# Two dozen tiles of a decoder kernel at other on-chip addresses: small tables regrouped, one 4-byte tile added

## The reference, cut to what matters

```python
def swiglu(x, w_gate, w_up, w_down):
    return (jax.nn.silu(x @ w_gate) * (x @ w_up)) @ w_down
def reference(...):
    mem_k, mem_v = split(rms_norm(mem, mem_norm) @ w_mem_kv)
    h = x
    h = h + mlstm_layer(rms_norm(h, ln_mix0), mem_k, mem_v, ...)
    h = h + swiglu(rms_norm(h, ln_ffn0), w_gate0, w_up0, w_down0)
    h = h + mla_layer(rms_norm(h, ln_mix1), positions, mem_k, mem_v, ...)
    h = h + moe_swiglu(rms_norm(h, ln_ffn1), w_router1, we_gate1, we_up1, we_down1)
    return h
```

## Time and profile before

| | |
|---|---|
| median of three executions | 1530.54 us (1529.33 to 1535.26) |
| the profiled execution | 1527.4 us, of which 1525.6 us from the first to the last instruction (the span) |
| TensorE products busy | 1464.8 us, 96% of the span |
| TensorE weight loads (beside the products) | 1221.0 us, 80% |
| VectorE | 1211.0 us, 79% |
| ScalarE | 1050.3 us, 69% |
| GpSimd | 40.8 us, 3% |
| moved by the DMA engines | 442.02 MB, mean 290 GB/s |
| granted TensorE clock, mean | 0.987 of full |

### The profile page before, as it was taken

How to read it: one execution, slowest core, us unless ns; L and a number is a source line. 1 busy time by engine, 2 the same in 40 slices (tenths; PEclk the granted TensorE clock), 3 DMA queues, 4 the chain that set the end, 5 groups by cost and what they waited for, 6 DMA issues and landing times.

```text
span 1525.6 us, 22113 instructions
## 1 busy us (share of the span) xinstructions
PE 1464.8 (96%) x7056; PEld 1221.0 (80%) x7056; DVE 1211.0 (79%) x1584; ACT 1050.3 (69%) x1395; POOL 40.8 (3%) x83
## 2 busy tenths in 40 slices
PE   6998999999988899999999999999999999999995
PEld 5987888888886788878878878888888888887883
DVE  6957655555565689989989989989988988998993
ACT  5664644444584377887787778878778778788772
POOL 1000000000000000000000010000000000000000
PEclk9999999999998999999999999999999999999997
DMA  8554365555242469999999999999999999999990
GB/s 270 165 180 138 139 220 182 186 195 162 66 166 77 172 240 384 378 355 387 377 351 382 390 350 386 384 360 373 380 384 346 393 381 352 389 377 350 396 393 34
DMA packets 191802, 442.02 MB, mean 290 GB/s; under 512 B 8750, under 2 KB 20364, under 8 KB 191756
## 3 DMA queue, kind: packets, MB, share of 16 engines
q1 hardware_dynamic: 188636, 429.90, 77.8%
q0 software_dynamic: 3120, 11.54, 2.7%
HBM read 433.54 MB, written 7.86 MB: 289 GB/s over the span
## 4 chain that ended last, share of the span: by engine, by line
PE 90%; DVE 5%; ACT 3%; issue 1%; DMA 0%; ACTq 0%; SPq 0%; DVEq 0%
PE bank L465 86%; PE bank L1025 2%; DVE w_lo L1613 1%; ACT w_hi L1130 1%; DVE xT_lo L1655 1%; DVE aT_lo L2274 0%; PE bank L751 0%; ACT aT_hi L1519 0%; PE bank L477 0%; DMA late<-in_mem_dram 0%; PE bank L656 0%; ACT scr L1467 0%; DVE stat L1634 0%; DVE stat L1632 0%; DVE stat L1633 0%
## 5 line engine op out<-in xcount | busy, mean ns | idle before, releaser
L1613 DVE TENSOR_TENSOR w_lo<-raw,w_hi 128x1024 fp32r<-128x1024 f32 (+1 forms) x832 | 958.6, 1197 | 175.5 <-ACT w_hi L1130 160.2
L1130 ACT ACTIVATE w_hi<-raw 128x1024 fp32r<-128x1024 f32 (+1 forms) x832 | 839.9, 1043 | 216.0 <-PE bank L465 210.8
L465 PE MATMUL bank<-w_hi,xT_hi 128*128 128x512 f32 (+4 forms) x1358 | 529.7, 390 | 12.3 <-DVE w_lo L1613 4.4
L465 PE MATMUL bank<-w_hi,xT_lo 128*128 128x512 f32 (+4 forms) x1358 | 521.8, 384 | 0.0
L465 PE MATMUL bank<-w_lo,xT_hi 128*128 128x512 f32 (+4 forms) x1358 | 521.2, 384 | 0.0
L465 PEld LDWEIGHTS bank<-w_hi,xT_hi 128*128 128x128 f32 x1358 | 255.9, 188 | 63.8 <-issue 8.6
L465 PEld LDWEIGHTS bank<-w_hi,xT_lo 128*128 128x128 f32 x1358 | 255.7, 188 | 49.6
L465 PEld LDWEIGHTS bank<-w_lo,xT_hi 128*128 128x128 f32 x1358 | 256.0, 189 | 46.0
L465 PE MATMUL bank<-w_hi,aT_hi 128*128 128x512 f32 x544 | 214.1, 394 | 5.8 <-DVE aT_lo L2274 5.8
L465 PE MATMUL bank<-w_lo,aT_hi 128*128 128x512 f32 x544 | 214.1, 394 | 0.0
L465 PE MATMUL bank<-w_hi,aT_lo 128*128 128x512 f32 x544 | 211.6, 389 | 0.0
(11 more groups left out here) (354 smaller groups left out, 763.0 us busy)
## 6 DMA issues: line engine op xcount, KB each, us to landing
raw<-in_we_gate_dram SPq DMA_DIRECT2D x112, 1024.0 KB, 7.7
raw<-in_we_up_dram SPq DMA_DIRECT2D x112, 1024.0 KB, 7.9
raw<-in_we_down_dram SPq DMA_DIRECT2D x112, 1024.0 KB, 6.9
raw<-in_w_gate_dram SPq DMA_DIRECT2D x14, 1024.0 KB, 5.1
raw<-in_w_up_dram SPq DMA_DIRECT2D x14, 1024.0 KB, 5.1
raw<-in_w_down_dram SPq DMA_DIRECT2D x14, 1024.0 KB, 4.8
raw<-in_w_in_dram SPq DMA_DIRECT2D x16, 768.0 KB, 4.9
raw<-in_w_out_dram SPq DMA_DIRECT2D x8, 1024.0 KB, 5.2
```

Source lines behind the costliest of these rows:

```text
L465: return pe.matmul(o, a, b, start=start, stop=stop, skip_group_check=True, **kw)
L1130: act.activation(split_piece(w_hi, c, shape, half), raw_piece(c, shape, half), ACT.Copy).then_inc(hi_ready, 1)
L1613: dve.tensor_tensor(split_piece(w_lo, c, shape, half), raw_piece(c, shape, half), F(split_piece(w_hi, c, shape, half)), ALU.subtract).then ...
```

## The change

Three small tiles (`row_no` of 12 bytes per partition, `gate_bias` and `pos_i` of 8) are declared later, behind `stat`; a tile `line_gap` of 4 bytes, which no instruction uses, is declared behind them; in layer 0's group `qk_in` goes to the end; in the experts' group `xg` and `y_out` go in front of `onehot`. No instruction is added, removed or moved: the lists of all engines are the same row for row in both programs, and only addresses in them differ.

```diff
-        row_no = sb("row_no", [P, TB + 1])
...
-        gate_bias = sb("gate_bias", [LH, 2])
-        pos_i = sb("pos_i", [P, TB], I32)
...
         stat = sb("stat", [P, 5, 40])
+        row_no = sb("row_no", [P, TB + 1])
+        gate_bias = sb("gate_bias", [LH, 2])
+        pos_i = sb("pos_i", [P, TB], I32)
+        sb("line_gap", [P, 1])
         kmT = sb("kmT", [P, 2, S])
...
-            qk_in = sb("qk_in", [P, 2, QB, S + TAPS - 1], scope=part)
             qkT = sb("qkT", [P, QKB, S], scope=part)
...
             headsel = sb("headsel", [LH, LH, P], scope=part)
+            qk_in = sb("qk_in", [P, 2, QB, S + TAPS - 1], scope=part)
...
             ys_lo = sb("ys_lo", [P, D], F32R, scope=part)
+            xg = sb("xg", [P, D], scope=part)
+            y_out = sb("y_out", [P, D], scope=part)
             onehot = sb("onehot", [P, TB, P], F32R, scope=part)
...
-            xg = sb("xg", [P, D], scope=part)
-            y_out = sb("y_out", [P, D], scope=part)
```

## The result

The changed kernel took 1537.46 us (median of 20 executions, 1534.47 to 1541.76), the kernel before 1530.4 us in 20 executions of the same session (1527.14 to 1535.26). The ratio is 1.0044, with a 95% interval of 1.0033 to 1.0055: 6.7 us, and not no change. The profiled execution took 1536.72 us, of which 1535.0 us is the span.

What follows compares the result with a forecast made beforehand. TensorE was taken to set the pace, with 90% of the chain. The terms summed to 0.0 us (-0.7 to +0.9, to +3 without slack), so the forecast was the earlier median, 1530.5 us, range 1526.5 to 1537.

Steps and rivals of the forecast that it cites:

- four kinds: All tiles: some stay, layer 0's big ones keep remainder 32, later ones go 0 to 32, small tables 32 to 0.
- what an instruction pays for a big operand at remainder 32: The one number the sum needs: at most 1 ns per TensorE load, -5 to +5 on VectorE, -14 to +10 on ScalarE.
- 40 ns of room hides them: Down products' 544 loads per term: 188 ns each beneath products starting 228 ns apart, so priced at 0.
- The pairs: Like operations on tiles at remainder 32 and 0 in the trace before (`gm`/`km`, `late`/`xr`): load difference at most 1 ns.
- Rest: Other loads 0.3 us; split operations hidden by 3.75 us of slack, else 2.8 us; layer 1's mixer 0.5 us; gather and scatter 0.
- Rival A: Weight loads from big tiles at remainder 32 run at half rate: 42 us more, 1572 us, 122 more at worst; chance 0.03.
- Rival B: Operands fetched in 64-byte units, so loads at remainder 32 touch nine, not eight: 6.3 us more, 1536.8 us; chance 0.03.
- Rival C: Per-partition scalars from tables at remainder 32 cost 15 ns more, now saved: 2.2 us less, 1528.3 us; chance 0.02.
- Rival D: Big tiles reach multiples of 64 after all, layer 0's going 32 to 0: worth 0, at most 0.3 us; chance 0.01.
- lines of 16 bytes: On-chip memory lines by the skill: starts at 32 and 0 cost the same, making the 64-byte-unit rival's 6.3 us nothing.

Runs made afterwards that it cites:

- e1: The changed kernel without the 4-byte tile, against the kernel before: 1530.65 us, ratio 0.9993.
- e4: The kernel before with a 4-byte tile ahead of `raw`, so every tile stands 32 bytes further: 1532.3 us, ratio 1.0004 to the kernel before.
- m1: TensorE alone, 784 products of the down product's form in 53 groups differing only in addresses: 226.7 ns for `xT`'s, 228.9 and 233.2 for `aT`'s before and after.
- m2: TensorE alone, 36 products per address group, then fp32 transpositions: 226.7 ns in step, 228.9 at 192 ahead, 233 to 234 at the rest; transpositions 109.2.
- m3: A measurement of address pairs with fewer columns and other number formats: 232.4 ns at 128 ahead; with 384 columns no price at 32.
- e3: The changed kernel with `aT_hi` and `aT_lo` alone back at their old remainder by 256: 1530.59 us, ratio 0.9996 to the kernel before.

## Why the prediction was wrong

- **Addresses and their four kinds: right.** The 4-byte tile does the reverse of the change's name, and without it the big tiles are where they were (e1). But that the sum needs "what an instruction pays for a big operand at remainder 32" was the wrong question. Moving every start by 32 bytes cost nothing (e4); the price belongs to the pair of weights and moving data.
- **"40 ns of room hides them": the step that failed.** I priced the loads of `aT_hi` and `aT_lo` at 0 since 188 ns of load fit beneath 228 ns between products. They still fit: the loads did not get longer. Yet the products start 4.3 ns further apart. A load that is covered in full is not therefore free: m1 has the same step, 228.9 to 233.2 ns, with nothing else at work. 1632 x 4.3 = 7.0 us was missing from the sum.
- **The sign of it stood in the trace before.** I used the mean of the earlier trace rows, 16.44 us for 72 products, as one pace. Split by the weights' tile it is 227.5 ns for `xT` (no distance by 256; 226.7 once settled) and 229.0 for `aT` (192 ahead). Two products of one form and unlike pace, on the engine that holds 90% of the chain, called for a reason.
- **The pairs were the wrong pairs.** `gm` against `km` and `late` against `xr` were read at the loads' lengths, with transpositions or 64 columns moving. m2 shows that transpositions pay nothing, and m3 that fewer columns pay less or nothing (down to 256; 64 was not tried). The pairs told the truth of their own forms and nothing of 512 columns.
- **Rest: right.** VectorE, ScalarE, the transpositions, gather and scatter at 0 (e3; L1026's loads 138 ns, `aT_lo`'s operation 692); `late`'s first transpositions still slow, 230 ns a load; waits in place. One count was off and changes nothing: layer 0's last step puts its turned block into `xT_hi` and `xT_lo`, so `aT_hi` and `aT_lo` are written 68 times and not 70.
- **Rival A: out.** Loads from `act_f` did not grow. **Rival B** gave 1536.8 us, near the measured 1537.5, but by luck, since its mechanism isn't there: the loads it wanted at 159 and 211 ns took 138 and 187, and transpositions stayed 108 to 109 ns apart. **Rival C: out**; `y_out`'s operation, with `gslot` now at 0, took 686 ns where C wanted 670 and the kernel before had 684. **Rival D** forecast no loss. Where the tiles lie on the chip no run shows, and e4 shows that 32 bytes more for all of them make no difference. The Trainium skill's lines of 16 bytes (SBUF — State Buffer, "Door 1: The DMA port swizzle") were taken to mean that a start at 32 costs as one at 0. For a tile by itself e4 and e3 agree; for weights beside moving data the measurement goes against that reading, 233.4 ns at 32 ahead to 226.7 at 0 (m2).
- **The chances.** The 0.90 stood for a move of less than 0.5%, and 0.44% lies within it; but the 20 executions of each kernel tell 0.33 to 0.55% from nothing, and 1537.46 us is 0.5 above the end of the range. That an address costs nothing, at 0.86, was wrong. It rested on pairs of other forms, none of the form that fills the chain.

## What to carry to other kernels

In a kernel that TensorE bounds, take the distance between starts of products of one form, split by the tile that the weights come from. If fp32r products with 512 columns differ (here 226.7, 228.9, 233.3 ns), compare the remainders by 256 of the two start addresses: equal ones, at multiples of 32, were the fastest, and a spare tile of 64 bytes bought 0.3%. With 256 columns the pair in step was the dearer one (m3), so measure the form that fills the chain. A start at a multiple of 64 bought nothing by itself (e4), and a 4-byte tile high up in the list of tiles moves all that follow.

## What the runs showed of the hardware

- fp32r, 128 x 128 weights, 512 columns, clock at its 2.4 GHz level (granted clock 1.00 in m2 from 46 to 269 us): 226.7 ns between starts at best, that is 544 cycles, and 233.3, 560 cycles, out of step; the row of the load itself keeps 187 to 188 ns either way.
- Where both streams move alike by 32 to 192 bytes, seven to ten distances of 224 to 236 ns come before it settles at 226.7 (m2). In the full kernel the first nine distances behind a change of the weights' tile have a mean of 229.1 ns (`xT`, before).
- bf16 with 512 columns (215.8 ns), fp32 (429 ns for each pass) and transpositions (109.2 ns) show no dependence (m3, m2).
- What in TensorE or the memory does this was not measured. That it is a meeting of the next weights' read with the moving read is an inference from the period of 256 bytes and from e4. Open, too, is why a run of products in step needs nine distances to settle, and what rules starts off multiples of 32.
